# Cached keys and values of two attention stages in eight 512 KB parts, three in flight, instead of four 1 MB parts issued at once

## The reference, cut to what matters

```python
# layer 0, samples (differential): 8 key heads of 64, 4 value heads of 128
bk_all = jnp.concatenate([c_bk, kb], axis=1)      # 2048 cached + 16 new
scores = jnp.einsum('bthed,bshed->bhets', q2, k2) * SCALE
attn = p[:, :, 0] - lam * p[:, :, 1]              # p: softmax over the masked scores
out = jnp.einsum('bhts,bshd->bthd', attn, v)
# layer 1, samples (forgetting): 16 heads of 64
scores = jnp.einsum('bthd,bshd->bhts', q, k) * SCALE
scores = scores + cq[..., :, None] - ck[..., None, :]
out = jnp.einsum('bhts,bshd->bthd', softmax(mask(scores)), v)
```

## Time and profile before

| | us |
|---|---|
| median of 3 runs (lowest, highest) | 3624.5 (3622.27, 3626.77) |
| the profiled execution, its own time | 3619.44 |
| its span, first to last instruction | 3617.7 |
| TensorE busy in the span | 3336.7 (92%) |
| VectorE, ScalarE, GpSimd busy | 1595.2, 1125.3, 254.4 |
| DMA moved | 493.21 MB, mean 136 GB/s |

### The profile page before, as it was taken

How to read it: one execution, slowest core, us unless ns; L and a number is a source line. 1 busy time by engine, 2 the same in 40 slices (tenths; PEclk the granted TensorE clock), 3 DMA queues, 4 the chain that set the end, 5 groups by cost and what they waited for, 6 DMA issues and landing times. The chain is left out here.

```text
span 3617.7 us, 63048 instructions
## 1 busy us (share of the span) xinstructions
PE 3336.7 (92%) x25000; PEld 2915.1 (81%) x25000; DVE 1595.2 (44%) x2913; ACT 1125.3 (31%) x2343; POOL 254.4 (7%) x338
## 2 busy tenths in 40 slices
PE   8997699798999999997899889999888999999997
PEld 7886577587999999996789766666677999999996
DVE  5427477463333333335231276676543333333334
ACT  4215355443211112113222155555533121121111
POOL 2310000032000000004000000000022000000003
PEclk9999799899999999999899999999989999999999
DMA  5436599443111111112554399899553111111112
GB/s 173 123 125 187 177 352 337 162 145 106 35 35 58 36 45 35 35 46 88 146 174 132 134 347 339 304 329 334 200 183 110 45 35 35 57 46 35 35 36 98
DMA packets 398384, 493.21 MB, mean 136 GB/s; under 512 B 68464, under 2 KB 250256, under 8 KB 398032
## 3 DMA queue, kind: packets, MB, share of 16 engines
q1 hardware_dynamic: 398176, 490.35, 40.7%
HBM read 407.10 MB, written 84.10 MB: 136 GB/s over the span
## 5 line engine op out<-in xcount | busy, mean ns | idle before, releaser
L2562 DVE TENSOR_TENSOR f_gated<-f_gated,f_up 128x384 f32<-128x384 f32 x132 | 73.1, 554 | 734.2 <-ACT f_gated L2492 734.2
L2586 DVE TENSOR_TENSOR f_y<-f_y,f_down 128x512 f32<-128x512 f32 x396 | 269.4, 686 | 229.5 <-PE f_down L2681 229.5
L2668 PE MATMUL f_gate<-m_ht_hi,f_w_hi 128*128 128x384 f32 x1056 | 355.0, 336 | 12.1 <-DVE f_w_lo L2613 12.1
L2668 PE MATMUL f_gate<-m_ht_lo,f_w_hi 128*128 128x384 f32 x1056 | 354.3, 336 | 0.0
L2668 PE MATMUL f_gate<-m_ht_hi,f_w_lo 128*128 128x384 f32 x1056 | 354.3, 336 | 0.0
L2668 PE MATMUL f_up<-m_ht_hi,f_w_lo 128*128 128x384 f32 x1056 | 352.7, 334 | 0.0
L2668 PE MATMUL f_up<-m_ht_hi,f_w_hi 128*128 128x384 f32 x1056 | 352.7, 334 | 0.0
L2668 PE MATMUL f_up<-m_ht_lo,f_w_hi 128*128 128x384 f32 x1056 | 352.7, 334 | 0.0
L2681 PE MATMUL f_down<-f_wo_hi,f_act_hi 128*128 128x512 f32 x792 | 313.1, 395 | 10.6 <-DVE f_y L2586 9.3
L2681 PE MATMUL f_down<-f_wo_lo,f_act_hi 128*128 128x512 f32 x792 | 309.7, 391 | 0.0
L2681 PE MATMUL f_down<-f_wo_hi,f_act_lo 128*128 128x512 f32 x792 | 309.4, 391 | 0.0
(11 more groups left out here) (404 smaller groups left out, 6804.5 us busy)
## 6 DMA issues: line engine op xcount, KB each, us to landing
jc_kc<-in_cache_c_k SPq DMA_DIRECT2D x64, 1024.0 KB, 10.8
jc_vc<-in_cache_c_v SPq DMA_DIRECT2D x64, 1024.0 KB, 8.8
jb_kc<-in_cache_b_k SPq DMA_DIRECT2D x32, 1024.0 KB, 11.8
jb_vc<-in_cache_b_v SPq DMA_DIRECT2D x32, 1024.0 KB, 9.1
m_raw<-in_w_ffn_in SPq DMA_DIRECT2D x44, 512.0 KB
f_raw<-in_w_ffn_in SPq DMA_DIRECT2D x44, 512.0 KB
f_raw_o<-in_w_ffn_out SPq DMA_DIRECT2D x22, 1024.0 KB, 6.1
m_raw<-x SPq DMA_DIRECT2D x18, 512.0 KB, 4.1
```

Of the source, the lines that this page charges most:

```text
L2562: dve.tensor_tensor(prod[:, b], silu[:, b], up[:, q, 0:gw], ALU.mult).then_inc(prod_done, 1)
L2586: dve.tensor_tensor(part, part, down[:, half, :], ALU.add).then_inc(added, 1)
L2668: last = pe.matmul(acc[:, q, 0:gw], a[:, s, k, u, :], b[:, k, token], start=(k == 0 and j == 0), stop=(k == KT - 1 and j == 2))
```

## The change

`parts` goes from 4 to 8, `per` from 4 to 2, and a part's load waits until the third part ahead of it has landed, for keys and for values alike. Nothing else is edited; the semaphore lists grow from 8 to 16 and from 4 to 8 with `parts`, and `range(0, 2 * per)` and `per * 2` now mean 4 tiles instead of 8.

```diff
-    parts, per = 4, PAST // 4 // P
+    parts, per, in_flight = 8, PAST // 8 // P, 3
...
                 for x in range(parts):
+                    if x >= in_flight:
+                        sp.wait_ge(kc_loaded[u % 2 * parts + x - in_flight], 16 * (u // 2 + 1))
                     sp.dma_start(kc[:, u % 2, 1 + per * x:1 + per * (x + 1)],
...
                 for x in range(parts):
+                    if x >= in_flight:
+                        sp.wait_ge(vc_loaded[x - in_flight], 16 * (u + 1))
                     sp.dma_start(vc[:, x], v_cache[stream_of(u), x * span:(x + 1) * span, columns_of(u)].rearrange(
```

## The result

The changed kernel takes 3677.7 us, median of four runs (3675.7 to 3683.8), against 3623.4 (3622.2 to 3626.8) for the kernel before on the same chip: 1.5% slower, ratio 1.0153 with a 95% interval of 1.0141 to 1.0165. The forecast was 3611, with a range up to 3646.

The account below looks back on a forecast made before the run. TensorE, busy 92% of the span, was taken to set the end, delayed by instruction fetches sharing the DMA engines. -24 + 1 + 2 + 7.5 = -13.5 us gave 3606, or 3611 in runs like those shown; range 3594 to 3646.

Parts of the forecast that it names:

- Does the queue still run full?: Throttled loads: three 512 KB parts in flight keep full rate with 0.11 us to spare per part; +1 us.
- The DMA rival: Joint stages: gaps of 0.5 us at ten waits make DMA the bound; about 3655 us, chance 0.13.
- Queued behind the new waits: SyncE's list: bias rows, new keys, store and next head come later but have cover, except at the opening.
- the sign of the DMA rival: Sign of a wrong forecast: TensorE or VectorE waiting for `jc_kc` or `jc_vc` DMAs.
- Fetches (-24 us): TensorE's instruction fetches meet a shorter queue: 15 of 18.3 us issue waits and -7 in `jc`, -2 in `jb`.
- the lines that were to be under 5: Sign of a right forecast: issue rows at L1552, L1575 and L1590 in `jc` under 5 us together.
- the 7 us that were hoped for: Part of the fetch gain in `jc`: half of TensorE's longer busy time and clock loss goes, -7 us.
- The prediction's 3.2 us for a part: Landing time of a 512 KB part estimated from the skill page's fit; three in flight would keep up.
- The openings (+1 and +1): Stage openings: head 1 is issued later, behind unit 0's throttled keys; +1 us each in `jb` and `jc`, 0 to +3.
- `per` in `turn_probs` (+7.5): Group 1 waits for the second half of the exponentials: 0.5 us in 15 units of `jc`, none in `jb`.
- the 0 for `attend_sample`: Half of 1.95 us of products moves from step 4 to step 5, same products in all; 0, from -3 to +3.

Follow-up runs that it names:

- the last kernel: Kernel before with four parts of 1 MB, two in flight, and the stores issued by GpSimd: 3617.4 us, ratio 0.9982.

## Why the prediction was wrong

**Does the queue still run full? (+1 us): the step that failed.** The sum took the landing time of a lone 1 MB transfer, the shortest of 64, and made 3.74 us for a part and "full rate with 0.11 us to spare". As a shortest time that was right: the quickest 512 KB part of `jc` in the changed kernel landed after 3.9 us. But with three under way the median is 5.6 for values and 5.9 for keys, so one part comes per 1.75 to 1.80 us, 0.4 us above the 1.36 of the wire. Over the 16 parts of a block that is 6.4 us, where the term had 0.05 to 0.5 us for each of ten waits, took +1 us in all, and had found only 2.6 us in hand. The warning stood in the same row, a median of 8.8 behind the 5.1. That median belongs to a queue of up to 4 MB, so it is too long for 1.5 MB, as the shortest is too short: (8.8 - 1.36) / 3 = 2.5 us a part from the one, 1.25 from the other, and the truth between them. The DMA rival, given 0.13, had this mechanism. Its 3655 does not follow from its own working, which found +26 us and then added 20; with 26 it is 3661. Both are below what came, as it left out the next point.

**"Queued behind the new waits": the store.** The prediction named "the store" in SyncE's list and then gave all of the list cover because of the head's. The two stores behind the values stand in none of its sentences. Nor did it follow a store to its waiter, `stored[j]`, which VectorE needs within the next block. This second failed step set where the loss first fell, 45.4 us in `jc` and 8.6 in `jb`, and with the stalls TensorE's lower clock: the windows above show 0.50 behind one of them, and its busy time in `jc` grew by 10.8 us. Moving the stores gave back 19 us and brought out the wait for values that the prediction had named as the sign of the DMA rival; so for the loss as a whole the rate is the cause, and the store the first place where it is paid.

**Fetches (-24 us): the direction held, the size did not.** Issue waits in `jc` went from 19.1 us to 10.3, and 7.1 of these at the lines that were to be under 5: -8.8 where 15 were forecast. Busy time did not fall by the 7 us that were hoped for but rose by 10.8. With the loss removed (2 MB in flight) the throttle is worth 5 to 8 us beside the kernel before (0.9978 to 0.9987) and about 10 beside the unthrottled eight parts (1.0014 less 0.9987).

That the waits are fetches of code, which the prediction inferred from the size of the packets, the traces do show. Before, 59 instruction packets came in `jc` from 2110 to 2600 us, one per 8.3 us on average, and each of the 15 issue waits there ended 1.2 to 1.5 us after the end of such a packet. The wait of the earlier trace rows lasts from 2344.73 to 2347.09, and the packet ran from 2344.59 to 2345.63. In the same stretch of all fourteen kernels together it is 168 of 168 waits, 1.2 to 1.7 us behind a packet. Before, 44 of the 59 packets have no such wait behind them. What the throttle does to the fetches stays open: the packets themselves take 1.0 to 1.1 us by their median in every kernel, however much is in flight. The waits do not simply follow the depth of the queue either: 2.0 us with 1 MB in flight and also with the keys alone throttled, but 18.5 with the values alone, 10.3 and 13.6 with 1.5 MB in flight, 13.7 to 19.9 with 2, 19.8 with 2.5, 17.2 with 3 and 19 to 21 unthrottled. Nor is their link to the time close: 19.9 us of them at 0.9982 in the last kernel, 2.0 at 1.0027 with the keys alone.

The Trainium skill (DMA: Bandwidth & Descriptors, "Rules for kernel authors") asks for at least 1 MiB per DMA. Parts of 512 KB held the rate of 1 MB parts here as long as 2 MB were in flight, so no run shows that rule at work. The prediction's 3.2 us for a part comes from a fit that stands in the same page's "Anatomy of one DMA — SWDGE (gpsimd) path" and is given for transfers issued by GpSimd, while SyncE issues these. It is below the shortest landing of such a part in any run here, 3.4 us, and by it three in flight would have kept up.

**The openings (+1 and +1).** TensorE's wait for head 1 in `jb` was 2.83 us; after:

```profile
PE jb_scores_a L1493 <- DMA jb_q_lo<-planes_ab: 4.5, 1, 4.5
```

+1.7. In `jc` the two opening waits went from 23.2 to 26.1 us, +2.9; both are within the 0 to 3 given.

**`per` in `turn_probs` (+7.5).** The wait is where it was said to be, in all 15 units of `jc`, beside the earlier trace rows:

```profile
2424.55 0.66 PE L1594 MATMUL jc_s_ps<-jc_ident,jc_s_scores 128*128 128x128 f32 x4 [0.35 <-ACT jc_s_scores L1732]
...
2424.30 0.20 ACT L1732 ACTIVATION_READ_ACCUMULATOR jc_s_scores<-jc_s_scores,jc_s_neg 128x1 f32 x1
```

It is 0.35 us instead of 0.5, 5.1 in all. The step alone cost 9 us (5 to 13), which holds the 7.5, and the 0 for `attend_sample` was not contradicted. With four parts in flight the same step cost nothing that shows.

## What to carry to other kernels

A throttle that lets N parts be in flight holds the rate to about N times the part's bytes over its landing time at that depth, as long as that is below what the queue can move. The shortest landing of an unthrottled run gives too good a rate and its median too bad a one, so measure at the depth in question; here 2 MB in flight kept the rate, 1.5 MB cost 1.5% of the time and 1 MB 6%. Before adding a wait to an engine that issues in order, write down its whole list from the code, odd and even blocks apart, and follow everything behind the wait to the one who waits for it, stores to whoever reuses their buffer too. And look where else a constant such as `per` stands before changing it for the sake of the loads.

## What the runs showed of the hardware

- The landing time of a 512 KB transfer depends on what is around it: 3.4 us at its shortest in any run, and by the median of the values in `jc` 4.9 with two in flight, 5.6 with three, 6.2 with four, 7.2 with five, 8.6 with eight.
- The spacing of parts stops falling between 1.5 and 2 MB in flight: 1.75 to 1.80 us per 512 KB at 1.5 MB, 1.44 to 1.58 from 2 MB on, with 512 KB and 1 MB transfers alike. At 1.5 MB the DMA share still reads 0.91 to 0.93 at 297 to 315 GB/s, so the share hardly shows the loss and GB/s does.
- Every wait ahead of a TensorE product in `jc` that the profile calls "issue", 168 in fourteen kernels, ends 1.2 to 1.7 us after the end of a 16 KB instruction packet. Before the change they are up to 2.6 us long.
- Less in the queue is also slightly better than all of it, 0.9978 to 0.9987 at 2 MB, 0.9994 at 2.5 and 1.0004 at 3. The gain is small and neighbouring intervals overlap. TensorE's fetch waits do not account for it: of the four kernels with 2 MB, three have 13.7 to 15.9 us of them and one 19.9, at the same ratio; the mechanism is not shown.
